# A hybrid decoder step: the order of loads, key and value requests and normalisations in the last stage of products

## What is computed

```python
hn = rmsnorm(x, norm_g[l])
u, g_main, q_mem, g_mem = split(hn @ w_in[l])
y = rglru(causal_conv(u))            # layer 0
y = sink_attend(rope(u), k, v, ...)  # layer 1: window of 128, shared k and v
om = mem_attend(q_mem, mem_k[l], mem_v[l])
z = concatenate([y * silu(g_main), om * silu(g_mem)])
x = x + z @ w_out[l]                 # z has 1536 columns
...
return rmsnorm(x, final_g), ...      # y_prompt, y_sample and the caches
```

## Time and profile before

| what | us |
|---|---|
| median of three runs (2051.12 to 2054.98) | 2054.16 |
| profiled execution, time | 2052.63 |
| profiled execution, span | 2050.7 |
| TensorE busy | 2023.9 (99%) |
| VectorE busy | 1307.4 (64%) |
| ScalarE busy | 951.8 (46%) |
| GpSimd busy | 276.3 (13%) |

### The profile page before, as it was taken

The page is one execution under the profiler, slowest core; times in us unless marked ns, Lnnn a source line. Parts: engine busy times, 40 slices in busy tenths (PEclk is TensorE's granted clock), DMA queues, the critical chain, the costliest instruction groups (busy, mean ns, idle before and its releaser), DMA issues.

```text
span 2050.7 us, 34924 instructions
## 1 busy us (share of the span) xinstructions
PE 2023.9 (99%) x14353; PEld 1603.6 (78%) x14353; DVE 1307.4 (64%) x2148; ACT 951.8 (46%) x2061; POOL 276.3 (13%) x249
## 2 busy tenths in 40 slices
PE   9999999999999999999999999999999999999998
PEld 7788887777777777777888888777787778788776
DVE  4845437888888753222634444588888888867667
ACT  5733335778778833222533333444444443423332
POOL 0000002221111100000100000222222330223321
PEclk9999999999999999999999999999999999999999
DMA  9421213443332674354211111222221224777784
GB/s 379 152 65 42 65 39 110 138 141 94 120 107 91 224 257 164 110 195 152 86 58 39 44 30 33 65 86 71 86 68 58 79 71 139 273 245 271 256 294 185
DMA packets 142080, 265.74 MB, mean 130 GB/s; under 512 B 15109, under 2 KB 78629, under 8 KB 137433
## 3 DMA queue, kind: packets, MB, share of 16 engines
q1 hardware_dynamic: 136704, 248.82, 35.5%
q10 hardware_dynamic: 5216, 14.69, 2.0%
HBM read 189.89 MB, written 73.65 MB: 129 GB/s over the span
## 4 chain that ended last, share of the span: by engine, by line
PE 92%; DVE 3%; DMA 2%; ACT 2%; issue 1%; POOL 0%; SPq 0%; ACTq 0%; DVEq 0%; POOLq 0%
PE bank L608 52%; PE bank L2101 12%; PE bank L2665 10%; PE bank L150 2%; PE bank L1174 2%; PE bank L712 2%; PE bank L448 2%; PE bank L1160 2%; PE bank L699 2%; PE bank L908 1%; PE bank L628 1%; DMA op_zraw<-z_scratch 1%; PE bank L702 1%; DVE in_x L348 1%; DMA mk_w<-in_w_mem_kv 0%
## 5 line engine op out<-in xcount | busy, mean ns | idle before, releaser
L608 PE MATMUL bank<-x_hi,w_hi 128*128 128x512 f32 x1600 | 636.0, 398 | 0.4 <-DVE w_lo L594 0.4
L608 PE MATMUL bank<-x_hi,w_lo 128*128 128x512 f32 x1600 | 624.0, 390 | 0.0
L608 PE MATMUL bank<-x_lo,w_hi 128*128 128x512 f32 x1600 | 623.1, 389 | 0.0
L608 PEld LDWEIGHTS bank<-x_hi,w_hi 128*128 128x128 f32 x1600 | 300.2, 188 | 96.6 <-issue 35.4
L608 PEld LDWEIGHTS bank<-x_hi,w_lo 128*128 128x128 f32 x1600 | 300.3, 188 | 64.4
L608 PEld LDWEIGHTS bank<-x_lo,w_hi 128*128 128x128 f32 x1600 | 300.6, 188 | 60.8 <-issue 0.7
L2101 PE MATMUL bank<-wo_hi,z_hi 128*128 128x512 f32 x384 | 152.3, 397 | 2.7 <-DVE z_lo L1824 1.2
L2101 PE MATMUL bank<-wo_lo,z_hi 128*128 128x512 f32 x384 | 149.7, 390 | 0.0
L2101 PE MATMUL bank<-wo_hi,z_lo 128*128 128x512 f32 x384 | 149.5, 389 | 0.0
L2665 PE MATMUL bank<-op_whi_p,op_zhi 128*128 128x512 f32 x336 | 136.2, 405 | 11.3 <-DVE op_x L2547 3.9
L758 DVE TENSOR_TENSOR it_P_lo<-bank,it_P_hi 128x512 fp32r<-128x512 f32 x64 | 41.2, 687 | 161.6 <-ACT it_P_hi L753 161.6
(11 more groups left out here) (367 smaller groups left out, 3264.0 us busy)
## 6 DMA issues: line engine op xcount, KB each, us to landing
w_raw<-in_w_items SPq DMA_DIRECT2D x25, 1024.0 KB, 5.1
z_scratch<-it_gz SPq DMA_DIRECT2D x96, 256.0 KB, 2.6
it_cs<-in_rope SPq DMA_DIRECT2D x32, 512.0 KB, 4.1
op_x<-x_scratch SPq DMA_DIRECT2D x32, 512.0 KB, 4.2
z_raw<-z_scratch SPq DMA_DIRECT2D x16, 768.0 KB, 5.0
op_zraw<-z_scratch SPq DMA_DIRECT2D x64, 192.0 KB, 5.5
in_rows<-in_x_prompt SPq DMA_DIRECT2D x4, 2048.0 KB, 26.5
in_x<-in_x_T SPq DMA_DIRECT2D x4, 2048.0 KB, 26.8
```

Source lines behind the costliest of these rows:

```text
L608: last = nc.tensor.matmul(ps, s_, r_, start=(k == 0 and q == 0), stop=(k == KT - 1 and q == 2))
```

## The change

- In the hooks of unit 0: the remainder of the last P3 chunk is made before the tokens' remainders of unit 1 instead of behind the attention's normalisation.
- SP: `load_z(3)` is issued before the loop; in the loop each unit issues the store of unit u-1, then load_z(u+2), then load_x(u+1). In unit 8 the samples' rows stand before load_z(10), the table and window behind load_x(9).
- Keys: the first four in unit 8 before the rounding of P7's weights (after product P6 of unit 7), the other four at the end of unit 8.
- Values: issued in unit 11 behind the rounded parts of unit 12 and ahead of step 2 of ScalarE, instead of at the end of unit 10.
- The normalisations of units 10 and 11 stand behind the additions of P1 and P4 instead of P2 and P1; some steps of the samples on VectorE and TensorE stand one or two products later.
- A wait for the window's loads is added on ScalarE before rows are copied into the window's values.

```diff
+    def sp_rows(s):        # waits and the 13 loads of rows, as in sp(s, 0) before
+    def sp_first(s):       # table and window, as in sp(s, 0) before
+    def sp_values(s, bs=range(NS)):   # values, as in sp(s, 2) before
...
         if step == 1:
             if l == 1:
                 s.wait_ge(rows_sum, n1 + 1)
+                s.wait_ge(win_ld, 32)
...
     def sync(s):
+        load_z(s, 3)
         for u in range(2, UNITS):
-            if u < UNITS - 1:
-                load_z(s, u + 1)
             if u <= 8:
                 store_x(s, u - 1)
             else:
                 store_y(s, u - 1)
+            if u == 8:
+                s.wait_ge(mmd, MM0 + NPROD * 8)
+                sm["sp_rows"](s)
+            if u < UNITS - 2:
+                load_z(s, u + 2)
             if u < UNITS - 1:
                 load_x(s, u + 1)
...
             if u == 8:
-                s.wait_ge(mmd, MM0 + NPROD * 8)
-                sm["sp"](s, 0)
+                sm["sp_first"](s)
...
             if u == 8:
+                act.wait_ge(mmd, MM0 + made(7, P6))
+                sm["sp_keys"](act, range(4))
                 weights_act(act, P7)
...
             if u == 8:
-                act.wait_ge(mmd, MM0 + NPROD * 8)
-                sm["sp_keys"](act)
+                sm["sp_keys"](act, range(4, NS))
             if u == 9:
                 sm["act"](act, 0)
                 sm["sp"](act, 1)
             if u == 10:
                 sm["act"](act, 1)
-                sm["sp"](act, 2)
             if u == 11:
+                sm["sp_values"](act)
                 sm["act"](act, 2)
...
         if q == 32:
             add(v, 0, P5)
+            v.wait_ge(whi, W0 + 1)
+            nc.vector.tensor_tensor(w_lo[0][P3][:, KQ - 1, :], ...)
             tokens_low(v, 1, 0)
...
+    norm_at = lambda u: (1, 2) if u in (11, 12) else (0, 1)
...
-                if u >= 9 and i < 2:
-                    norm(v, c, u - 1, i)
+                if u >= 9 and i in norm_at(u):
+                    norm(v, c, u - 1, norm_at(u).index(i))
...
-                step = {(9, 6): 0, (10, 5): 1, (11, 2): 2, (12, 1): 3, (12, 5): 4, (13, 2): 5}.get((u, i))
+                step = {(9, 6): 0, (10, 5): 1, (11, 3): 2, (12, 1): 3, (13, 0): 4, (13, 4): 5}.get((u, i))
...
-                step = {..., (11, 6): (3, 3), (12, 3): (4, 3), (13, 0): (5, 3)}.get((u, i))
+                step = {..., (11, 6): (3, 3), (12, 5): (4, 3), (13, 2): (5, 3)}.get((u, i))
```

More of the change, by code:

```diff
@@ L1449, in samples, with sp_keys @@
         W4, W5 = m.bank[4], m.bank[5]
-    def sp_keys(s):
-        for b in range(NS):
+    def sp_keys(s, bs=range(NS)):
+        for b in bs:
             s.dma_start(kb[b][:, :, :], A["cache_mem_k"][l, b]).then_inc(k_ld, 16)
@@ L1456, in sp @@
         if step == 0:
[L1457 to L1473, removed]
+            sp_rows(s)
+            sp_first(s)
         if step == 2:
-            s.wait_ge(sc_d, n1 + 1)
-            for b in range(NS):
-                s.dma_start(vb[b][:, :, :], A["cache_mem_v"][l, b].rearrange("(t p) h d -> p t (h d)", p=128)).then_inc(v_ld, 16)
+            sp_values(s)
         if step == 1:
@@ L1497, in sp @@
             s.wait_ge(win_out, 32)
+    def sp_rows(s):
+        it["rows_all_stored"](s)
+        s.wait_ge(*it["after"]("z_ready", NI * NCH))
+        it["z_all_stored"](s)
+        for w in range(NW):
+            n, step_ = (2, NS) if w == 0 else (4, 32)
+            s.dma_start(rows[place(w):place(w) + NS, 0:n, :],
+                        m.srow_d[0:n * step_, 256 * w:256 * w + 256].rearrange("(j r) c -> r j c", r=step_)[0:NS]).then_inc(rows_ld, 16)
+    def sp_first(s):
+        if l == 0:
+            for q, w in enumerate(("lru_wa", "lru_wx")):
+                for r in range(2):
+                    s.dma_start(bd[64 * r:64 * r + 64, :, q, :], A[w][0].rearrange("(k r) c d -> r c k d", r=2)[r]).then_inc(gate_ld, 16)
+            s.dma_start(outs["conv_s"][0, :, 0:2, :], A["state_conv"][0, :, 1:3, :]).then_inc(st_out, 16)
+        else:
+            s.dma_start(cs[:, :], A["rope_s"]).then_inc(win_cs, 16)
+            s.dma_start(kw[:, :, :], A["cache_win_k"]).then_inc(win_ld, 16)
+            s.dma_start(vw[:, :, :], A["cache_win_v"]).then_inc(win_ld, 16)
+    def sp_values(s, bs=range(NS)):
+        s.wait_ge(sc_d, n1 + 1)
+        for b in bs:
+            s.dma_start(vb[b][:, :, :], A["cache_mem_v"][l, b].rearrange("(t p) h d -> p t (h d)", p=128)).then_inc(v_ld, 16)
     def pool(g):
@@ L1722, in dve @@
                 nc.vector.tensor_copy(states[0:20, 512 * i:512 * i + 512], m.bank[6 + i][0:20, :]).then_inc(st_e, 1)
-    return dict(signals=signals, sp=sp, sp_keys=sp_keys, pool=pool, pe=pe, act=act, dve=dve, sum_rows=sum_rows, z2=z2, zs_r=zs_r, zs_0=nz, st_e=st_e if l == 0 else None)
+    return dict(signals=signals, sp=sp, sp_keys=sp_keys, sp_rows=sp_rows, sp_first=sp_first, sp_values=sp_values, pool=pool, pe=pe, act=act, dve=dve, sum_rows=sum_rows, z2=z2, zs_r=zs_r, zs_0=nz, st_e=st_e if l == 0 else None)
 def output(nc, m, sem, l, A, outs, it, sm, prior=None):
@@ L2567, in within_dve @@
             add(v, 0, P5)
+            v.wait_ge(whi, W0 + 1)
+            nc.vector.tensor_tensor(w_lo[0][P3][:, KQ - 1, :], w_raw[0][P3][:, KQ - 1, :], w_hi[0][P3][:, KQ - 1, :].bitcast(F32), ALU.subtract).then_inc(wlo, 1)
             tokens_low(v, 1, 0)
@@ L2577, in behind_dve @@
         if q == 32:
-            v.wait_ge(whi, W0 + 1)
-            nc.vector.tensor_tensor(w_lo[0][P3][:, KQ - 1, :], w_raw[0][P3][:, KQ - 1, :], w_hi[0][P3][:, KQ - 1, :].bitcast(F32), ALU.subtract).then_inc(wlo, 1)
             tokens_low(v, 1, 1)
@@ L2686, in tensor @@
                     product(pe, u, i)
-                step = {(9, 3): (0, 1), (10, 1): (1, 1), (10, 2): (1, 2), (10, 3): (1, 3), (11, 1): (2, 3), (11, 6): (3, 3), (12, 3): (4, 3), (13, 0): (5, 3)}.get((u, i))
+                step = {(9, 3): (0, 1), (10, 1): (1, 1), (10, 2): (1, 2), (10, 3): (1, 3), (11, 1): (2, 3), (11, 6): (3, 3), (12, 5): (4, 3), (13, 2): (5, 3)}.get((u, i))
                 if step:
```

## The result

The changed kernel takes 2060.55 us (median, 2057.22 to 2062.97) against 2054.62 us for the kernel before beside it (2051.12 to 2059.36): ratio 1.0026, 95% interval 1.0016 to 1.0036. It is **slower by 0.26%**, outside the range of 2042.5 to 2057. Its profiled execution took 2061.82 us with a span of 2059.9, so the traces differ by 9.2 us where the medians differ by 5.9: places and waits are read from the traces, sizes from the ratios.

The account below looks back on a forecast made before the run. TensorE was taken as the bound, busy 99% of the span, so only its idle and slow clock could be won. Terms -4.2 + 1.3 - 2.3 - 0.4 - 6.0 + 7.4 gave -4.2 us: 2050.0 us, range 2042.5 to 2057.

Parts of the forecast that it names:

- step 1: Units 0 and 1: last block's remainder ahead of the tokens' removes a TensorE wait, leaving 1.45 us idle next: -4.2 us.
- step 2: Unit 8: P5's weights, asked for later, delay ScalarE and then GpSimd's P3 remainders: +1.3 us (0 to +4).
- step 3: Unit 9: earlier parts of unit 10 shorten the wait before unit 10; later x rows cost nothing: -2.3 us.
- step 4: Unit 10: first slow-clock stretch goes, a 1.4 us wait for an addition and a 1.6 us fall come: -0.4 us.
- step 5: Unit 11: later normalisation and values end the wait for ScalarE's squares; later exponentials cost 0.6: -6.0 us.
- step 6: Unit 12: x rows land late behind values and stores, 4.5 us idle plus 2.9 of slow clock: +7.4 us.
- Rival B: Units 9 and 12: strict order of asking makes both units' x rows late; +5.6 us in all, 2059.8; chance 0.12.
- Rival A: Unit 12: queues take turns, x rows pass the values, landing T11+21; +1.5 instead of +7.4, 2044.1; chance 0.27.

Follow-up runs that it names:

- e1: Kernel before with only the remainder of unit 0's last P3 chunk moved ahead of unit 1's token remainders: 2048.76 us, ratio 0.9977 to the kernel before.
- e6: Changed kernel with unit 7's weight requests for P3 and P5 ahead of unit 9's token parts: 2054.42 us, ratio 1.0002 to the kernel before.
- e11: Changed kernel with only the second four keys asked for in unit 9: 2054.16 us, ratio 1.0001 to the kernel before.
- e12: Changed kernel with only unit 9's x row requests moved ahead of the sample rows: 2053.50 us, ratio 0.9996 to the kernel before.
- e8: Kernel before with the P3 remainder ahead and the normalisation of units 10 and 11 one addition later: 2045.89 us, ratio 0.9956 to the kernel before.
- e7: Changed kernel with P3's and P5's requests ahead of unit 9's parts, all keys in unit 9, values ahead of the exponential: 2050.20 us, ratio 0.9977 to before.
- e9: Changed kernel with SP's old order, window loads behind unit 10's parts, all keys in unit 9, values ahead of the exponential: 2044.45 us, ratio 0.9949 to before.
- e10: Changed kernel with SP's request order alone put back as before: 2051.92 us, ratio 0.9985 to the kernel before.

## Why the prediction was wrong

Unit by unit, from starts of first products in the two profiled executions (before: T8 = 1893.06, T9 = 1907.85, T10 = 1926.57, T11 = 1952.23, T12 = 1974.09, T13 = 1994.13, up to 0.4 us from those of the prediction; after: T8 = 1888.93, T9 = 1907.53, T10 = 1932.49, T11 = 1958.47, T12 = 1973.59, T13 = 2003.17):

| stretch | forecast | measured |
|---|---|---|
| before unit 8 (step 1) | -4.2 | -4.1 |
| unit 8 (step 2) | +1.3 | +3.8 |
| unit 9 (step 3) | -2.3 | +6.2 |
| unit 10 (step 4) | -0.4 | +0.3 |
| unit 11 (step 5) | -6.0 | -6.7 |
| unit 12 (step 6) | +7.4 | +9.5 |
| sum | -4.2 | +9.0 |

**Step 1 held**, in the place and size of what is late next too (1.41 for 1.45 us); e1 has it alone.

**Step 2 was mis-sized**, and came near its upper end. P5 was asked for at 1884.84 and took 10.1 us; the step took the 6.9 of the earlier trace rows. Parts of 9 and x rows, asked for within 7.6 us ahead of it, were still under way; in the trace of before the parts stood behind it. All of ScalarE's work of unit 8 came 2.8 us later than forecast (T8 + 6.1, not 3.3), TensorE stood 2.37 us, and 8 matmuls ran at the slow clock. GpSimd's remainders of P3, which the step named as the late ones, were not waited for; VectorE, which was to "keep up, just", did not: its addition stood behind P5's remainders. e6 shows that the place of P5's request is the cause.

**Step 3 is the step that failed**: "now behind four keys and the parts ... No cost". The parts' side went roughly as said (the wait on line 2547 is 1.66 us, for 1.05 forecast and 3.20 before). The x rows did not: they were asked for at T8 + 12.9 instead of 9, since the last part of unit 10 ahead of them waits for unit 8's fourth product, which the stall and the slow clock delayed; all eight keys were ahead of them; and SP's queue had a quarter of the bandwidth from 1903 to 1909. They landed at T8 + 27.8 where 17.5 was forecast and 19.2 allowed. e11 halves the second cause alone, and the wait goes: at T8 + 21.2 they are just in time. Rival B had this stall, by strict order and behind four keys, at 4.7 us; the place and near enough the size (5.63) were right and e12 refutes its rule. That its time, 2059.8, lies near the measured 2060.55 is luck: it left unit 8 at +1.3.

**Step 4** came out by cancellation. The wait for the addition was 0.23 us and not 1.4. The fall of the clock behind the tiny matmuls came (1939.65), and a second one that was not forecast (1946.16), which took in the product with the keys: 4.29 us for 3.66 before.

**Step 5 held.** No wait of VectorE on ScalarE's squares is left in unit 11, and the 0.6 us put down for the later exponentials did not come. The part of it that is the normalisation's alone is 2.4 of the 6.7 us (e8).

**Step 6 was right in mechanism**: the values asked for at T11 + 4.7 to 9.0, the stores behind them (7.6 and 7.2 us for the two that the rows wait for), then the x rows from T11 + 14.5, landed at T11 + 25.3; forecast 24, needed 20.15. The rows were 1.3 us later and TensorE was there 0.7 us sooner, so the idle was 6.60 for 4.5; the slow clock cost 2.8 for 2.9. Rival A did not come about, although its rule did. It gave the rows the landing of before, T11 + 21, as if the other queue cost them nothing; but from 1970 to 1984 SP's queue moved 3.1 MB against 2.5 MB of the other, 1212 packets to 1287, so it had 0.22 of the 0.40 MB/us.

What stays open: why in e7 the clock fell behind waits of 1.78 and 1.99 us and in e9 not behind one of 1.73; and how much of unit 8's delay is turns with the keys and how much the parts ahead of P5, since e6 moves both at once.

## What to carry to other kernels

Before a load is moved behind others, list what **both** queues have under way and the packet size of each: a queue of small packets gets the smaller share of bytes, and a load with 2 us of slack behind 4 MB of another queue's has none. To hold a request back, put it behind something that it must wait for, not behind a few microseconds of work on its engine; and don't put that wait ahead of work that is due. When several stalls are to be taken away, don't add up their lengths from one trace: e7 was expected at a span of 2036 to 2038 and had 2050.7, because waits of 1.8 to 3.3 us came up in other units and the clock fell behind them.

## What the runs showed of the hardware

- Two hardware queues took turns by packets in stretches of 385 to 410 GB/s: 231 to 232, 236 to 237, 354 to 357, 144 to 144 in 2 to 3 us each, while the bytes were 0.84 to 0.32 MB in the first. At 285 to 302 GB/s (1898 to 1901) the counts were 214 to 105.
- ScalarE's queue issued requests 4 us ahead of an activation that precedes them in the program (eighth key 1898.87, activation 1902.97).
- Idle cost more than its length: 5.63 and 6.60 us were followed by 3.9 and 5.1 us at 1.2 GHz. The length alone did not decide it: 1.41 us (unit 1), 1.66 us (unit 10's start) and 1.73 us (e9, unit 11) were followed by no slow matmul, 1.95 us (e10, unit 10) by 7, and 0.23 us behind 16 tiny matmuls (line 1545, unit 10) by 6.
